# Splitting a norm's output into high and low parts: scale taken into the first product, the low part made on VectorE in one step

## The chip, the cores and the metric

The kernel runs on one core of a Trainium2 chip. The metric is the device time of one execution in microseconds (us). The core's engines run side by side and wait for one another by semaphores: TensorE (PE in the profile; PEld is its weight load), VectorE (DVE), ScalarE (ACT), GpSimd (POOL), and SyncE (SP), whose queue issues most DMAs.

## The reference, cut to what matters

The program is two transformer-like blocks over 512 tokens of width 1024 (256 of context, 256 of the sequence); the second block works on 256 tokens. All arithmetic is float32. What the change touches are the norms:

```python
def _rms_norm(x, gain):
    y = x * lax.rsqrt(jnp.mean(x * x, axis=-1, keepdims=True) + EPS)
    return y * gain

def _modulated_norm(h, gain, shift, scale):      # first block, 6 times
    return _rms_norm(h, gain) * (1.0 + scale) + shift

# second block, 3 times: rms_norm(h, norm_mix), rms_norm(h, norm_xattn), rms_norm(h, norm_mlp)
```

Each norm's output is multiplied by a large weight matrix (or several).

## The kernel before, in words

A float32 product is made of three TensorE products of rounded parts. Every operand `x` is kept as a high part `hi` (x rounded to the fp32r type) and a low part `lo = x - hi`; `three()` adds weights_lo·x_hi, weights_hi·x_lo and weights_hi·x_hi in PSUM (lines 231 to 233 of the profile). Weights come from memory in units of 512 KB (8 tiles of 128x128), issued by SyncE into 3 landing buffers; ScalarE makes their high part (`feed_act`, L214) and GpSimd their low part (`feed_pool`, L224), up to 4 units ahead of TensorE.

Data are held feature-major: 8 slices `d` of 128 features each, with 512 (or 256) tokens along the free axis. `linear()` starts a product with the first 1, 2 or 4 output tiles (`first`) slice by slice: for each `d` TensorE waits until slice `d` of the norm's low part is ready, and does 3 x `first` matmuls on it. The other output tiles follow without waiting for the norm. So the norm and the start of the next product overlap, at the pace of the slower.

A norm of 512 tokens goes like this. ScalarE squares, VectorE adds the squares, TensorE sums over features, ScalarE takes the root, VectorE the reciprocal (L492), and TensorE spreads the inverse root over all partitions into a PSUM bank (`spread_pe`, L469); it then does a few matmuls of no use (`busy_pe`, L420) that keep it occupied. From there, per slice `d`:

- VectorE `norm_x_dve` (L498): work = x * inverse root, 512 wide, one operand in PSUM
- ScalarE `norm_act` (L485): hi = work * scale + shift, in two halves (context tokens and sequence tokens have their own scale and shift)
- VectorE `norm_z_dve` (L504): work = work * scale + shift, in two halves, in SBUF
- GpSimd `norm_pool` (L520): lo = work - hi, 512 wide; TensorE waits for this

VectorE runs them in the order x0 x1 x2 z0 x3 z1 ... x7 z5 z6 z7 (`norm_dve`). The six norms of the first block (`norm00`, `norm01`, `norm02`, `norm10`, `norm11` on 512 tokens, `norm12` on 256) have a scale and a shift. The three of the second block (`norm mix`, `norm xattn`, `norm mlp`, 256 tokens) have a gain and no shift, so their pieces are one 256-wide piece. `norm00` is written out by hand in `start_dve`: its x products are made while the scale and shift themselves are still being computed from streamed weights (`ada_dve`); z follows when they are there. `norm_pool` sits in GpSimd's program between two stretches of `feed_pool`.

## Time and profile before

| | |
|---|---|
| time, median of 3 runs | 2959.94 us (2954.56 to 2963.52) |
| the profiled execution | 2956.96 us, span 2955.0 us |
| TensorE busy | 2811.4 us (95%) |
| VectorE busy | 1540.9 us (52%) |
| ScalarE busy | 1186.2 us (40%) |
| GpSimd busy | 1543.2 us (52%) |
| DMA | 381 MB, mean 129 GB/s |

"Busy" counts the time in which an engine executes instructions. The chain that ended last goes back from the last instruction, at each step to what released it; it lies on TensorE for 82% of the span. Matmuls are pipelined, so a row's duration (0.39 us for a 128x512 matmul) is longer than the distance from its start to that of the next. The chain is read together with the waits, which say for what an engine stood idle.

### The profile page before, as it was taken

To read this page: it belongs to the slowest core of one execution; us is meant where nothing else is said; L and a number is where in the kernel's file an instruction comes from. 1 tells how busy PE (TensorE), PEld (TensorE's weight loads), DVE (VectorE), ACT (ScalarE), POOL (GpSimd) and SP (SyncE) were. 2 spreads that over 40 slices of the span, in tenths; PEclk is the share of its full clock that TensorE was granted. 3 is DMA by queue.
4 is the path that set the end of the run, shared out by engine and by line. 5 is a ranking of instruction groups with operands and counts; after the bars stand their busy time and mean duration, and the time that the engine had idled before them with its cause. 6 is when DMAs were issued, how large, how long until landed. Compare 5 with 4: busy or idle time off the path is not lost.

```text
span 2955.0 us, 52281 instructions
## 1 busy us (share of the span) xinstructions
PE 2811.4 (95%) x21638; PEld 2427.7 (82%) x21638; DVE 1540.9 (52%) x2922; ACT 1186.2 (40%) x2076; POOL 1543.2 (52%) x861
## 2 busy tenths in 40 slices
PE   7999999988889999999999998999998998998999
PEld 5888878877777788887888885799997898997999
DVE  4777235535554667316665136554284865723570
ACT  4222234324453322223222244544445465544553
POOL 4444453343324544444444452388884565696697
PEclk9999999999999999999999998999998999999999
DMA  6555322210001555324554225155553343354365
GB/s 256 203 198 200 99 76 82 89 58 3 4 3 51 174 176 178 128 93 144 178 182 156 93 89 100 57 195 190 173 186 101 109 142 108 108 164 136 116 199 164
DMA packets 106123, 381.05 MB, mean 129 GB/s; under 512 B 11392, under 2 KB 16800, under 8 KB 104608
## 3 DMA queue, kind: packets, MB, share of 16 engines
q1 hardware_dynamic: 87456, 310.60, 32.2%
q10 hardware_dynamic: 18432, 67.12, 6.5%
q8 instruction: 172, 2.82, 0.4%
q14 instruction: 63, 0.52, 0.1%
HBM read 373.47 MB, written 4.19 MB: 128 GB/s over the span
## 4 chain that ended last, share of the span: by engine, by line
PE 82%; DVE 8%; POOL 3%; ACT 3%; issue 2%; DMA 1%; SPq 0%; ACTq 0%; DVEq 0%
PE bank L231 23%; PE bank L232 22%; PE bank L233 22%; POOL weights_lo L224 2%; PE bank L822 2%; DVE norm_work L504 1%; PE upper_banks L1555 1%; DVE norm_work L498 1%; PE upper_banks L231 1%; PE upper_banks L232 1%; PE upper_banks L233 1%; DMA ada_first<-w_ada 1%; DVE square_sums L451 1%; PE bank L919 1%; PE upper_banks L838 1%
## 5 line engine op out<-in xcount | busy, mean ns | idle before, releaser
L224 POOL TENSOR_TENSOR weights_lo<-weights_landing,weights_hi 128x1024 fp32r<-128x1024 f32 x554 | 1338.5, 2423 | 1101.0 <-ACT weights_hi L214 1100.4
L214 ACT ACTIVATE weights_hi<-weights_landing 128x1024 fp32r<-128x1024 f32 x554 | 586.5, 1061 | 1235.2 <-PE bank L233 1112.7
L231 PE MATMUL bank<-normed_hi,weights_lo 128*128 128x512 f32 (+1 forms) x2664 | 912.2, 342 | 17.6 <-POOL normed_lo L520 11.9
L232 PE MATMUL bank<-normed_lo,weights_hi 128*128 128x512 f32 (+1 forms) x2664 | 900.9, 338 | 0.0
L233 PE MATMUL bank<-normed_hi,weights_hi 128*128 128x512 f32 (+1 forms) x2664 | 900.0, 338 | 0.0
L231 PEld LDWEIGHTS bank<-normed_hi,weights_lo 128*128 128x128 f32 x2664 | 502.3, 189 | 95.2 <-POOL normed_lo L520 27.6
L233 PEld LDWEIGHTS bank<-normed_hi,weights_hi 128*128 128x128 f32 x2664 | 502.1, 188 | 61.6
L232 PEld LDWEIGHTS bank<-normed_lo,weights_hi 128*128 128x128 f32 x2664 | 502.6, 189 | 58.4
L231 PE MATMUL bank<-hidden_hi,weights_lo 128*128 128x512 f32 (+1 forms) x960 | 329.1, 343 | 0.0
L232 PE MATMUL bank<-hidden_lo,weights_hi 128*128 128x512 f32 (+1 forms) x960 | 329.1, 343 | 0.0
L233 PE MATMUL bank<-hidden_hi,weights_hi 128*128 128x512 f32 (+1 forms) x960 | 329.1, 343 | 0.0
L572 DVE TENSOR_TENSOR hidden_lo<-silus,hidden_hi 128x512 fp32r<-128x512 f32 (+1 forms) x88 | 210.9, 2397 | 87.3 <-ACT hidden_hi L559 87.3
L625 DVE SCALAR_TENSOR_TENSOR residual<-bank,gate,residual 128x256 f32<-128x256 f32 x80 | 35.5, 479 | 358.3 <-PE bank L233 358.3
L231 PEld LDWEIGHTS bank<-hidden_hi,weights_lo 128*128 128x128 f32 x960 | 180.1, 188 | 24.3
L232 PEld LDWEIGHTS bank<-hidden_lo,weights_hi 128*128 128x128 f32 x960 | 180.1, 188 | 24.2
L233 PEld LDWEIGHTS bank<-hidden_hi,weights_hi 128*128 128x128 f32 x960 | 180.1, 188 | 24.2
L390 DVE CUSTOM_DVE_ANT_0 ada_products<-ada_rows,upper_banks,k_cond_pack 128x1024 f32<-128x1024 f32 x128 | 163.3, 1276 | 22.9 <-DMA ada_rows<-w_ada_rows 14.0
L390 DVE CUSTOM_DVE_ANT_0 ada_rows<-ada_rows,upper_banks,k_cond_pack 128x1024 f32<-128x1024 f32 x128 | 163.1, 1274 | 0.0
L570 DVE TENSOR_TENSOR silus<-silus,bank 128x512 f32<-128x512 f32 (+1 forms) x88 | 54.7, 621 | 183.7 <-PE bank L233 158.7
L520 POOL TENSOR_TENSOR normed_lo<-norm_work,normed_hi 128x512 fp32r<-128x512 f32 (+1 forms) x72 | 76.6, 1068 | 75.1 <-DVE norm_work L504 75.1
L1689 DVE SCALAR_TENSOR_TENSOR upper_banks<-gl,k_pack,upper_banks 128x255 f32<-128x255 f32 (+14 forms) x210 | 99.3, 473 | 7.4
L451 DVE TENSOR_TENSOR square_sums<-square_sums,squares 128x512 f32<-128x512 f32 (+1 forms) x48 | 67.3, 1402 | 35.9 <-ACT squares L443 35.9
(447 smaller groups left out, 3912.1 us busy)
## 6 DMA issues: line engine op xcount, KB each, us to landing
weights_landing<-w_up SPq DMA_DIRECT2D x176, 512.0 KB, 3.5
ada_rows<-w_ada_rows ACTq DMA_DIRECT2D x128, 512.0 KB, 4.3
weights_landing<-w_down SPq DMA_DIRECT2D x88, 512.0 KB, 3.4
weights_landing<-w_dn SPq DMA_DIRECT2D x33, 512.0 KB, 3.4
weights_landing<-w_mlp_up SPq DMA_DIRECT2D x32, 512.0 KB, 3.4
weights_landing<-w_mlp_down SPq DMA_DIRECT2D x32, 512.0 KB, 3.5
weights_landing<-w_gate SPq DMA_DIRECT2D x24, 512.0 KB, 3.4
weights_landing<-w_xbc SPq DMA_DIRECT2D x24, 512.0 KB, 3.5
```

Source lines behind the costliest of these rows:

```text
L214: k.nc.scalar.activation(k.WH[:, u % SLOTS, :], k.W[:, u % LANDS, :], ACT.Copy).then_inc(*k.AC.mark(("unit hi", u)))
L224: k.nc.gpsimd.tensor_tensor(k.WL[:, u % SLOTS, :], k.W[:, u % LANDS, :], k.WH[:, u % SLOTS, :].bitcast(F32), ALU.subtract).then_inc(*k.PO. ...
L231: nc.tensor.matmul(out, ll, rh, start=start, stop=False, skip_group_check=True)
L232: nc.tensor.matmul(out, lh, rl, start=False, stop=False, skip_group_check=True)
L233: return nc.tensor.matmul(out, lh, rh, start=False, stop=stop, skip_group_check=True)
L390: nc.vector.tensor_tensor_reduce(k.row[r % ROW_LANDS][:] if c else k.row_out[:], k.row[r % ROW_LANDS][:], k.upper[:, c * D:(c + 1) * D], 1 ...
L451: k.nc.vector.tensor_tensor(s, s, k.sq[:, d % 2, 0:tokens], ALU.add).then_inc(*k.DV.mark((st, "sum", d)))
L520: k.nc.gpsimd.tensor_tensor(lo(d), work(d), hi(d).bitcast(F32), ALU.subtract).then_inc(*k.PO.mark((st, "lo", d)))
L570: nc.vector.tensor_tensor(s, s, k.B[(2 * p + 1) % 4][:, 0:tokens], ALU.mult).then_inc(*k.DV.mark((st, "raw", p)))
L572: nc.vector.tensor_tensor(lo(p), s, hi(p).bitcast(F32), ALU.subtract).then_inc(*k.DV.mark((st, "lo", p)))
L822: mm = k.nc.tensor.matmul(bank[block(to), at + c * BLK:at + (c + 1) * BLK], lhs(rows, to, c), rhs(rows, to, c), start=True, stop=True)
L1689: nc.vector.scalar_tensor_tensor(y[:, a:LAT], x[:, 0:LAT - a], w[:, at, j:j + 1], y[:, a:LAT], ALU.mult, ALU.add).then_inc(*k.DV.mark(("co ...
```

## The change

For norms with scale and shift: VectorE's first step becomes work = (x * scale) * inverse root, in two halves, as one instruction each with the scale as a per-partition operand. ScalarE's high part is work + shift, and is marked and waited for by half. VectorE then makes the low part itself, (work + shift) - hi, as one instruction for each half; z is gone. GpSimd's program waits in that place until the last low part is made, and does nothing for the norm. VectorE's order is s0 s1 low0 s2 low1 ... s7 low6 low7. TensorE waits for VectorE's mark instead of GpSimd's (`norm_ready`).

For the three norms without shift: VectorE's first step takes the gain in, ScalarE rounds work, z is gone, and GpSimd makes lo = work - hi as soon as hi is there.

For `norm00` the products are no longer made ahead of the scale; all of it starts when the first scale is ready.

```diff
-def norm_act(k, act, st, work, hi, parts, when=None):
+def norm_act(k, act, st, work, hi, parts):
     for d in range(KT):
-        act.wait_ge(*k.DV.after(st, "x", d))
         for n, (a, b, scale, shift) in enumerate(parts):
-            k.nc.scalar.activation(hi(d)[:, a:b], work(d)[:, a:b], ACT.Identity, scale=scale(d),
-                                   bias=shift(d) if shift else 0.0).then_inc(...)
+            act.wait_ge(*k.DV.after(st, "scaled", d, n))
+            k.nc.scalar.activation(hi(d)[:, a:b], work(d)[:, a:b], ACT.Identity,
+                                   bias=shift(d) if shift else 0.0).then_inc(*k.AC.mark((st, "hi", d, n)))

-def norm_x_dve(k, dve, st, d, src, work, tokens, bank=5):
+def norm_scaled_dve(k, dve, st, d, src, work, parts, bank=5):
     if d == 0:
         dve.wait_ge(*k.PE.after(st, "spread"))
-    k.nc.vector.tensor_tensor(work(d), src(d), k.B[bank][:, 0:tokens], ALU.mult).then_inc(*k.DV.mark((st, "x", d)))
-
-def norm_z_dve(k, dve, st, d, work, parts):
-    dve.wait_ge(*k.AC.after(st, "hi", d))
     for n, (a, b, scale, shift) in enumerate(parts):
-        k.nc.vector.tensor_scalar(work(d)[:, a:b], work(d)[:, a:b], scale(d), shift(d) if shift else None, ALU.mult,
-                                  *((ALU.add,) if shift else ())).then_inc(...)
+        k.nc.vector.scalar_tensor_tensor(work(d)[:, a:b], src(d)[:, a:b], scale(d), k.B[bank][:, a:b], ALU.mult,
+                                         ALU.mult).then_inc(*k.DV.mark((st, "scaled", d, n)))
+
+def norm_low_dve(k, dve, st, d, work, hi, lo, parts):
+    for n, (a, b, scale, shift) in enumerate(parts):
+        dve.wait_ge(*k.AC.after(st, "hi", d, n))
+        k.nc.vector.scalar_tensor_tensor(lo(d)[:, a:b], work(d)[:, a:b], shift(d), hi(d)[:, a:b].bitcast(F32), ALU.add,
+                                         ALU.subtract).then_inc(...)

-def norm_dve(k, dve, st, src, work, tokens, parts, bank=5):
+def norm_dve(k, dve, st, src, work, hi, lo, tokens, parts):
     norm_r_dve(k, dve, st, tokens)
-    for d in range(KT + 2):
+    for d in range(KT + 1):
         if d < KT:
-            norm_x_dve(k, dve, st, d, src, work, tokens, bank)
-        if d >= 2:
-            norm_z_dve(k, dve, st, d - 2, work, parts)
+            norm_scaled_dve(k, dve, st, d, src, work, parts)
+        if d and st in MODULATED:
+            norm_low_dve(k, dve, st, d - 1, work, hi, lo, parts)
+
+MODULATED = ("norm00", "norm01", "norm02", "norm10", "norm11", "norm12")

 def norm_pool(k, pool, st, work, hi, lo):
+    if st in MODULATED:
+        pool.wait_ge(*k.DV.after(st, "lo", KT - 1))
+        return
     for d in range(KT):
-        pool.wait_ge(*k.DV.after(st, "z", d))
+        pool.wait_ge(*k.AC.after(st, "hi", d, 0))
         k.nc.gpsimd.tensor_tensor(lo(d), work(d), hi(d).bitcast(F32), ALU.subtract).then_inc(*k.PO.mark((st, "lo", d)))
...
     ada_dve(k, dve, 1)
-    for d in range(KT):
-        norm_x_dve(k, dve, "norm00", d, src, work, TOK)
     for u in range(2, ADA_FIRST):
         ada_dve(k, dve, u)
+    dve.wait_ge(*k.DV.after("ada scale", 0, 0))
     for d in range(KT):
-        norm_z_dve(k, dve, "norm00", d, work, modulated(k, 0, 0))
+        norm_scaled_dve(k, dve, "norm00", d, src, work, modulated(k, 0, 0))
+        if d:
+            norm_low_dve(k, dve, "norm00", d - 1, work, hi, lo, modulated(k, 0, 0))
+    norm_low_dve(k, dve, "norm00", KT - 1, work, hi, lo, modulated(k, 0, 0))
```

## Rows read from the trace of the kernel before

**Rows 1.** The page, part 1: busy time (share of the span) and instructions of each engine.

```profile
PE 2811.4 (95%) x21638; PEld 2427.7 (82%) x21638; DVE 1540.9 (52%) x2922; ACT 1186.2 (40%) x2076; POOL 1543.2 (52%) x861
```

**Rows 2.** Waits of PE: line waited for: us in total, times, longest.

```profile
PE bank L231 <- POOL normed_lo L520: 11.9, 26, 3.7
```

**Rows 3.** Stretches: length, busy time (instructions) per engine, PEclk the granted clock.

```profile
37.00:55.00 18.00, 14.86 (x65) 11.65 (x66) 12.04 (x16) 11.38 (x20) 14.23 (x10) 0.83 0.00 1
55.00:413.00 358.00, 358.00 (x1537) 287.60 (x1536) 197.81 (x260) 94.58 (x115) 155.23 (x65) 1.00 0.49 169
```

**Rows 4.** Timeline of DVE in norm01: start, length, engine, line, form, [idle before <-releaser].

```profile
417.64 1.88 DVE L498 TENSOR_TENSOR norm_work<-residual,upper_banks 128x512 f32<-128x512 f32 x3 [0.74 <-PE upper_banks L469]
419.50 0.73 DVE L504 TENSOR_SCALAR norm_work<-norm_work,scale,mod 128x256 f32<-128x256 f32 x2
420.75 1.30 DVE L504 TENSOR_SCALAR norm_work<-norm_work,scale,mod 128x256 f32<-128x256 f32 x2
```

**Rows 5.** Timeline of ACT and of POOL in norm01.

```profile
418.37 4.05 ACT L485 ACTIVATE normed_hi<-norm_work,mod,scale 128x256 fp32r<-128x256 f32 x8 [1.68 <-DVE norm_work L498]
...
420.31 1.27 POOL L520 TENSOR_TENSOR normed_lo<-norm_work,normed_hi 128x512 fp32r<-128x512 f32 x1 [8.73 <-DVE norm_work L504]
...
432.74 1.28 POOL L520 TENSOR_TENSOR normed_lo<-norm_work,normed_hi 128x512 fp32r<-128x512 f32 x1 [0.23 <-DVE norm_work L504]
```

**Rows 6.** Timeline of PE in norm01: occupying matmuls, slice 1, slice 7.

```profile
417.44 3.19 PE L420 MATMUL upper_banks<-k_cond_pack 128*128 128x256 f32 x14
...
423.47 0.50 PE L231 MATMUL bank<-normed_hi,weights_lo 128*128 128x512 f32 x1 [0.16 <-POOL normed_lo L520]
423.81 0.39 PE L232 MATMUL bank<-normed_lo,weights_hi 128*128 128x512 f32 x1
424.04 0.40 PE L233 MATMUL bank<-normed_hi,weights_hi 128*128 128x512 f32 x1
...
434.07 0.50 PE L231 MATMUL bank<-normed_hi,weights_lo 128*128 128x512 f32 x1
```

**Rows 7.** Timeline of DVE elsewhere: 256-wide three-operand instructions, PSUM source, then SBUF only.

```profile
2577.46 3.21 DVE L2219 SCALAR_TENSOR_TENSOR mem<-mem,k_pack,upper_banks 128x256 f32<-128x256 f32 x8
...
2265.83 1.52 DVE L1689 SCALAR_TENSOR_TENSOR cv<-gl,k_pack,cv 128x255 f32<-128x255 f32 x3
```

**Rows 8.** Timelines of DVE and PE in norm00.

```profile
36.67 0.18 DVE L345 SCALAR_TENSOR_TENSOR scale<-mod,k_cond_pack 128x16 f32<-128x16 f32 x1
...
40.15 0.79 PE L231 MATMUL bank<-normed_hi,weights_lo 128*128 128x512 f32 x1 [3.72 <-POOL normed_lo L520]
...
51.72 0.50 PE L231 MATMUL bank<-normed_hi,weights_lo 128*128 128x512 f32 x1
```

**Rows 9.** Timelines of DVE and PE in norm12 (256 tokens).

```profile
1907.14 1.08 DVE L498 TENSOR_TENSOR norm_work<-residual,upper_banks 128x256 f32<-128x256 f32 x3 [0.80 <-PE upper_banks L469]
...
1916.00 0.28 PE L231 MATMUL bank<-normed_hi,weights_lo 128*128 128x256 f32 x1
```

**Rows 10.** Timelines of DVE and POOL in norm mix (no shift).

```profile
2099.33 1.08 DVE L498 TENSOR_TENSOR norm_work<-residual,upper_banks 128x256 f32<-128x256 f32 x3 [0.52 <-PE upper_banks L469]
...
2100.76 0.72 POOL L520 TENSOR_TENSOR normed_lo<-norm_work,normed_hi 128x256 fp32r<-128x256 f32 x1 [3.88 <-DVE norm_work L504]
...
2105.59 2.22 POOL L520 TENSOR_TENSOR normed_lo<-norm_work,normed_hi 128x256 fp32r<-128x256 f32 x3 [0.23 <-DVE norm_work L504]
```

**Rows 11.** Timelines of POOL and PE in norm xattn (no shift).

```profile
2663.18 9.48 POOL L224 TENSOR_TENSOR weights_lo<-weights_landing,weights_hi 128x1024 fp32r<-128x1024 f32 x4 [2.09 <-ACT weights_hi L214]
...
2679.91 11.81 POOL L224 TENSOR_TENSOR weights_lo<-weights_landing,weights_hi 128x1024 fp32r<-128x1024 f32 x5
...
2682.33 0.50 PE L231 MATMUL bank<-weights_hi,mem_lo 128*128 128x512 f32 x1 [2.39 <-POOL weights_lo L224]
```

**Rows 12.** Timeline of PE around and after norm mlp (no shift).

```profile
2770.63 1.03 PE L420 MATMUL upper_banks<-k_cond_pack 128*128 128x256 f32 x4
...
2795.18 0.36 PE L231 MATMUL bank<-normed_hi,weights_lo 128*128 128x256 f32 x1 [0.68 <-POOL weights_lo L224]
```

**Rows 13.** Groups by form: a low part made on DVE inside the MLPs, count | busy, mean ns | idle.

```profile
L572 DVE TENSOR_TENSOR hidden_lo<-silus,hidden_hi 128x512 fp32r<-128x512 f32 x66 | 158.1, 2395 | 62.9 <-ACT hidden_hi L559 62.9
```

More of the change, by code:

```diff
@@ L517, in norm_pool, with norm_ready @@
+def norm_ready(k, st):
+    return lambda d: (k.DV if st in MODULATED else k.PO).after(st, "lo", d)
 def norm_pool(k, pool, st, work, hi, lo):
+    if st in MODULATED:
+        pool.wait_ge(*k.DV.after(st, "lo", KT - 1))
+        return
     for d in range(KT):
[L519 removed]
+        pool.wait_ge(*k.AC.after(st, "hi", d, 0))
         k.nc.gpsimd.tensor_tensor(lo(d), work(d), hi(d).bitcast(F32), ALU.subtract).then_inc(*k.PO.mark((st, "lo", d)))
@@ L691, in delta_pe @@
     linear(k, pe, st, "w_dn", DN_TILES, KT, lambda d: (k.n_hi[:, d, :], k.n_lo[:, d, :]), TOK, freed,
-           lambda d: k.PO.after("norm01", "lo", d), first=2, beside=beside)
+           norm_ready(k, "norm01"), first=2, beside=beside)
 def delta_act(k, act):
@@ L1706, in glu_pe @@
     freed = lambda n: None if n < 8 else k.AC.after("glu", "sig", (n - 8) // 2) if n % 2 else k.DV.after("glu", "ev", (n - 8) // 2)
-    linear(k, pe, "glu", "w_glu", 2 * KT, KT, both2(k), LAT, freed, lambda d: k.PO.after("norm mix", "lo", d), first=4, banks=8)
+    linear(k, pe, "glu", "w_glu", 2 * KT, KT, both2(k), LAT, freed, norm_ready(k, "norm mix"), first=4, banks=8)
 def glu_act(k, act):
@@ L2277, in cross_vq_pe @@
     linear(k, pe, "cross q", "w_xq", KT, KT, both2(k), LAT,
-           lambda n: k.AC.after("cross q", "ev", n - 4) if n >= 4 else k.AC.after("cross v", n // 2, n % 2), lambda d: k.PO.after("norm xattn", "lo", d),
+           lambda n: k.AC.after("cross q", "ev", n - 4) if n >= 4 else k.AC.after("cross v", n // 2, n % 2), norm_ready(k, "norm xattn"),
            first=1, beside=lambda n: cross_beside_pe(k, pe, n))
@@ L2469, in mlp2_pe @@
     freed = lambda n: k.DV.after("up2", "square", n - 8) if n >= 8 else None
-    linear(k, pe, "up2", "w_mlp_up", 4 * KT, KT, both2(k), LAT, freed, lambda d: k.PO.after("norm mlp", "lo", d), first=4, banks=8)
+    linear(k, pe, "up2", "w_mlp_up", 4 * KT, KT, both2(k), LAT, freed, norm_ready(k, "norm mlp"), first=4, banks=8)
     out_pe(k, pe, "down2", "w_mlp_down", 4 * KT, lambda d: (k.mh_hi[:, d, :], k.mh_lo[:, d, :]), LAT,
@@ L2540, in mlp_pe @@
     hi, lo = hidden(k, tokens)
-    up_pe(k, pe, st, "w_" + up, lambda d: (k.n_hi[:, d, a:TOK], k.n_lo[:, d, a:TOK]), tokens, lambda d: k.PO.after(norm, "lo", d))
+    up_pe(k, pe, st, "w_" + up, lambda d: (k.n_hi[:, d, a:TOK], k.n_lo[:, d, a:TOK]), tokens, norm_ready(k, norm))
     out_pe(k, pe, st + " down", "w_" + down, FT, lambda d: (hi(d), lo(d)), tokens, down_freed(k, st, st + " down"), down_ready(k, st), stat=after)
@@ L2625, in pe_program @@
     spread_pe(k, pe, "norm11", TOK)
-    window_project_pe(k, pe, swa, lambda d: k.PO.after("norm11", "lo", d), lambda n: None)
+    window_project_pe(k, pe, swa, norm_ready(k, "norm11"), lambda n: None)
     window_heads_pe(k, pe, swa)
@@ L2651, in pe_program, with norm_of_act @@
     mlp2_pe(k, pe)
-def norm_of_act(k, act, st, tokens, where, parts, when=None):
+def norm_of_act(k, act, st, tokens, where, parts):
     src, work, hi, lo = where
     rms_act(k, act, st, tokens)
-    norm_act(k, act, st, work, hi, parts, when)
+    norm_act(k, act, st, work, hi, parts)
 def act_program(k, act):
@@ L2662, in act_program @@
     start_act(k, act)
-    norm_act(k, act, "norm00", *first_norm(k, TOK)[1:3], modulated(k, 0, 0), k.DV.after("ada scale", 0, 0))
+    norm_act(k, act, "norm00", *first_norm(k, TOK)[1:3], modulated(k, 0, 0))
     mlp_act(k, act, "mlp00")
@@ L2700, in norm_of_dve @@
     src, work, hi, lo = where
-    norm_dve(k, dve, st, src, work, tokens, parts)
+    norm_dve(k, dve, st, src, work, hi, lo, tokens, parts)
 def dve_program(k, dve):
```

5 lines of the change are left out of this document (1 added, 4 removed).

## The prediction

> **What bounds the kernel now.** I read the page first: TensorE is busy for 95% of the span [rows 1]. Then the stretches: from one norm to the next it has no gap at all, 358.00 us busy of 358.00 [rows 3], so a norm that ends earlier moves everything behind it forward. Nothing there runs on a clock of its own: weights, their high and low parts and their DMAs are all released by work that moves too. Then the waits: TensorE waits for GpSimd's low part of a norm 26 times, 11.9 us in all [rows 2]. That understates what a norm costs, since a matmul behind a wait also starts its successor late: 0.34 us later (423.47 to 423.81) where the next pair is 0.23 apart [rows 6]. So I went to the timelines of the norms, where the end of the last slice decides, not the sum of waits.
>
> In norm01 VectorE's first x starts at 417.64 [rows 4], GpSimd's last low part ends at 432.74 + 1.28 = 434.02 [rows 5], and TensorE begins slice 7 at 434.07 [rows 6]. Eight slices took 16.4 us. The two z of a slice last 0.73 us when GpSimd is idle and 1.30 when it works [rows 4]: VectorE and GpSimd take turns, so x (0.60), the z pair and GpSimd's 1.27 to 1.28 don't overlap freely and a slice costs about 1.84 us. TensorE needs only 6 x 0.233 = 1.40 us for a slice, 1.51 if it had to wait for it. This pattern stands four times in the trace, at norm01, norm02, norm10 and norm11; the other norms are shorter.
>
> **Norms of 512 tokens with shift (four).** Removed: 8 x, 16 z on VectorE, 8 low parts on GpSimd. Added: 32 VectorE instructions of three operands, 256 wide. Their price: eight of this kind with a PSUM source took 3.21 us [rows 7]; with about 0.47 us for one alone this is (3.21 − 0.47)/7 = 0.391 us from start to start. With both tensors in SBUF three took 1.52 us [rows 7], (1.52 − 0.48)/2 = 0.52 apart, but each of those needs the result of the one before. In the new order no instruction needs its predecessor, so I take 0.391 for both kinds, and keep 0.52 as the upper end. For the lower end I have no row below 0.391 for this form.
>
> The last low part then ends at 31 x 0.391 + 0.47 = 12.6 us after the start, at 430.2 instead of 434.0. ScalarE doesn't hold it up: its halves come every 0.505 us (8 in 4.05, rows 5), 1.01 per slice against 1.56 from VectorE, and the first high half is there at 417.64 + 0.47 + 0.04 + 0.59 = 418.7, before the first low part wants it at 417.64 + 4 x 0.391 = 419.2. What is late next is TensorE itself. The first slice's low part is there at 417.64 + 5 x 0.391 + 0.47 = 420.1, but the occupying matmuls run to about 420.45 [rows 6]. From there blocks cost 1.40 where the wait is already met and 1.51 where not; VectorE delivers every 1.56. Followed slice by slice, slice 7 begins at 431.0 and ends at 432.4; before it ended at 434.07 + 0.11 + 1.40 = 435.6. Gain 3.1 us each, 12.4 us for four. Bounds: if waits cost TensorE nothing, 3.6 each; with 0.52 per instruction the last low part comes at 417.64 + 16.6 = 434.2, gain −0.2 each. GpSimd's new wait holds only its weight units, and it ends when the last low part ends, earlier than its own last low part did; ScalarE's weight units come behind its high parts, as before.
>
> The Trainium skill's page "VectorE: DVE Perf Modes", sections "The perf-mode tier table" and "Rules for kernel authors", speaks against the edit: a one-source float32 tensor_scalar runs two elements per cycle in SBUF, two-source ones one, and one should minimise the number of instructions. Its measured formula (N+151)/0.96 would make each new instruction 424 ns and the last low part end at 13.6 us, not 12.6; the gain of a norm would be about 2.8 us instead of 3.1.
>
> **norm00.** Here the 8 x were already hidden, and the products now come behind the scale, which is ready at 36.67 + 0.18 = 36.85 [rows 8]. That costs nothing only because the order is short: the first slice's low part ends at 36.9 + 2.4 = 39.3, TensorE started at 40.15 [rows 8]. VectorE ends at 36.9 + 12.6 = 49.5; TensorE began slice 7 at 51.72. TensorE's granted clock is 0.83 over this stretch [rows 3]: it has been idle before, and its first matmul takes 0.79 us [rows 8]. I let that slow start move along with it. Then TensorE gains the 0.75 us of the start and about 0.35 of waits later: 1.1 us. Bounds 0.3 to 1.9; at 0.52 per instruction it would lose 36.9 + 16.6 − 51.7 = 1.8.
>
> **norm12** (256 tokens, two VectorE instructions per slice). s0 at 1907.14 [rows 9], high part until 1908.24, low0 until 1908.75, then 0.78 per slice; the last low part waits for its high part and ends at about 1914.2. TensorE's own blocks with a wait are 0.81, so slice 7 begins at 1914.5 instead of 1916.00 [rows 9]. Gain 1.5 us (1.0 to 1.7).
>
> **The three norms without shift.** z goes, GpSimd starts behind the high part. norm mix: first low part at 2099.33 + 0.47 + 0.04 + 0.51 + 0.08 = 2100.43 instead of 2100.76 [rows 10]; TensorE needs 12 matmuls a slice and is then the slower one, gain 0.3. GpSimd's steps are 0.74 apart where VectorE leaves it alone (three in 2.22, rows 10) and were 0.97 with z between. norm xattn: GpSimd's weight units end at 2672.66, its eight low parts then take 5.9 us, to 2678.6 instead of 2679.91; TensorE stands idle 2.39 us for exactly the weight unit that follows [rows 11]. Gain 1.3, up to 2.4 if the next waits shrink too. norm mlp: TensorE's occupying matmuls run to about the time at which it starts the product, nothing there; its wait of 0.68 us at 2795.18 [rows 12] hangs on GpSimd's weight units, which come 1.5 us earlier. I take 0.3 (0 to 0.7).
>
> **Sum.** 12.4 + 1.1 + 1.5 + 0.3 + 1.3 + 0.3 = 16.9 us. The profiled execution took 2956.96 (span 2955.0 and 1.96 around it), so 2940.1. The median of the runs is 3.0 us higher, which gives 2943.0. I forecast 2941.
>
> **The rivals.**
> 1. *The new instructions don't overlap* (0.48 apart or more, as in the dependent rows). At 0.48 the last low part ends 15.4 us after the start: 1.0 us gained in each of four norms, 0.6 lost in norm00, 0.6 gained in norm12, 1.9 in the others, 6 in all: 2952. For it: the 0.52 of the SBUF form [rows 7], and the waits in front of every low part. Against: the waits are met long before.
> 2. *VectorE is held off by GpSimd* (slower). A low part on VectorE reads two SBUF tensors; the same subtraction in the MLPs lasts 2395 ns on average, while GpSimd makes weight parts [rows 13]. If GpSimd had weight work during a norm, a slice would cost 4 x 1.4 = 5.6 us (two low parts at 2.4, two products at 0.4) and a norm 8 x 3.8 = 30 us more: with five such norms about 3100. It decides from the first weight unit that GpSimd makes inside a norm. Against: GpSimd has been idle 8.73 us when the norm needs it [rows 5], and the new wait keeps it idle until the last low part.
> The Trainium skill's page "SBUF — State Buffer", section "Who interferes with whom", has the rule: a VectorE instruction with two SBUF inputs and a GpSimd one that reads SBUF exclude each other for a whole instruction. By that rule the trace agrees with the 2395 ns of rows 13, and the change is safe only through GpSimd's wait.
> 3. *TensorE pays nothing for its waits, and the weight supply behind the norms profits more*: 4 x 3.6 + 1.5 + 1.7 + 0.5 + 2.4 + 0.7 = 21, giving 2937.
> 4. *The gain is given back* in the stages that wait for GpSimd, ScalarE or DMA: a third of it lost, 2947 to 2952.
>
> **How the numbers follow.** Forecast 0.68; rival 1 0.12; rival 2 0.04; rival 3 0.08; rival 4 0.05; something slower that I don't see 0.03. Runs of one kernel spread by about 4.5 us around the median. The range 2933 to 2953 takes in the forecast with this spread, rival 3, and most of rivals 1 and 4. A measurement can tell 0.3%, 8.9 us, from no change; the line for faster is 2951. Faster: forecast, rival 3, half of rival 4 and a little of rival 1, 0.80. Same: 0.14. Slower: 0.06.
>
> **What would show it.** Right: in norm01 32 three-operand instructions about 0.39 apart, the last ending 12.6 us after the first; TensorE's slice 7 about 13.4 us after VectorE's start instead of 16.4; no GpSimd instruction inside a norm with shift; TensorE's wait before the weight unit of norm xattn down from 2.39 to about 1.1. Wrong: starts 0.48 or more apart; any low part near 2.4 us; or the norms shorter as forecast and the span not.

## The result

The kernel after takes 2942.10 us, median of 4 runs (2938.66 to 2946.09), the kernel before 2959.51 (2954.56 to 2963.52). The ratio is 0.9942, with a 95% interval of 0.9922 to 0.9963. The profiled execution took 2943.61 us, its span is 2941.5, 13.5 us less than before. The interval ends below 1: the kernel after is faster, by 0.4 to 0.8%.

The page of after, part 1, beside [rows 1]: VectorE has 34 us less to do and GpSimd 60; TensorE has the same matmuls and stands idle less.

```profile
PE 2813.5 (96%) x21638; PEld 2435.2 (83%) x21638; DVE 1506.7 (51%) x2938; ACT 1177.8 (40%) x2076; POOL 1483.2 (50%) x813
```

The groups of after by form (line, engine, form, count | busy, mean ns | idle before) show what a norm is now made of. ScalarE makes the high parts; on VectorE one kind of instruction is left, twice.

```profile
L483 ACT ACTIVATE normed_hi<-norm_work,mod 128x256 fp32r<-128x256 f32 x88 | 39.9, 503 | 30.9 <-DVE norm_work L497 30.9
L504 DVE SCALAR_TENSOR_TENSOR normed_lo<-norm_work,mod,normed_hi 128x256 fp32r<-128x256 f32 x88 | 38.4, 478 | 0.4 <-ACT normed_hi L483 0.4
L497 DVE SCALAR_TENSOR_TENSOR norm_work<-residual,scale,upper_banks 128x256 f32<-128x256 f32 x88 | 38.0, 474 | 3.5 <-PE upper_banks L469 3.5
```

The waits of TensorE in after, which answer to [rows 2] (11.9 us in 26 waits for the low part). Of the waits long enough for this list (over 0.15 us) one is left, and it is norm00's start.

```profile
PE bank L231 <- DVE normed_lo L504: 3.0, 1, 3.0
```

norm01 in the timelines of after (start, length, engine, line, form), VectorE first, which answers to [rows 4].

```profile
419.04 1.66 DVE L497 SCALAR_TENSOR_TENSOR norm_work<-residual,scale,upper_banks 128x256 f32<-128x256 f32 x4 [0.74 <-PE upper_banks L469]
420.62 0.88 DVE L504 SCALAR_TENSOR_TENSOR normed_lo<-norm_work,mod,normed_hi 128x256 fp32r<-128x256 f32 x2
421.41 0.87 DVE L497 SCALAR_TENSOR_TENSOR norm_work<-residual,scale,upper_banks 128x256 f32<-128x256 f32 x2
...
430.07 1.67 DVE L504 SCALAR_TENSOR_TENSOR normed_lo<-norm_work,mod,normed_hi 128x256 fp32r<-128x256 f32 x4
```

ScalarE and GpSimd in the same norm [rows 5]. GpSimd makes nothing here: it stood for 18.85 us, and its weight units go on when the last low part is made.

```profile
419.56 1.71 ACT L483 ACTIVATE normed_hi<-norm_work,mod 128x256 fp32r<-128x256 f32 x4 [1.47 <-DVE norm_work L497]
...
431.82 7.15 POOL L224 TENSOR_TENSOR weights_lo<-weights_landing,weights_hi 128x1024 fp32r<-128x1024 f32 x3 [18.85 <-DVE normed_lo L504]
```

TensorE [rows 6]: the occupying matmuls, the first matmul of the product, the starts of slices 6 and 7, and the first matmul behind slice 7.

```profile
418.84 3.19 PE L420 MATMUL upper_banks<-k_cond_pack 128*128 128x256 f32 x14
421.68 0.58 PE L231 MATMUL bank<-normed_hi,weights_lo 128*128 128x512 f32 x1
...
431.00 0.50 PE L231 MATMUL bank<-normed_hi,weights_lo 128*128 128x512 f32 x1
...
432.50 0.39 PE L231 MATMUL bank<-normed_hi,weights_lo 128*128 128x512 f32 x1
...
433.91 0.39 PE L231 MATMUL bank<-normed_hi,weights_lo 128*128 128x512 f32 x1
```

The reading is simple. VectorE's instructions start 0.394 us apart (four from 419.04 to 420.62), and the last low part ends at 430.07 + 1.67 = 431.74, 12.70 us after the first start; before it was 16.4. Slice 7 starts 13.46 us after VectorE's start and is done at 14.87 us, against 17.9 before (slice 7 began at 434.07, and with 0.11 + 1.40 us for a block that had to wait, the prediction's price, it was done at 435.6). A first matmul of 0.50 us marks a block that had to wait a little; slice 7 begins with one of 0.39, so its data were there.

**Where the 17 us went.** The kernel's stages can be measured from one norm's spread (L469) to the next. Two such stages in the timeline of TensorE, before:

```profile
952.09 0.65 PE L469 MATMUL upper_banks<-k_cond_pack,rr 128*128 128x128 f32 x4
...
1334.45 0.65 PE L469 MATMUL upper_banks<-k_cond_pack,rr 128*128 128x128 f32 x4 [0.20 <-DVE rr L492]
```

and after:

```profile
948.75 0.65 PE L469 MATMUL upper_banks<-k_cond_pack,rr 128*128 128x128 f32 x4
...
1328.01 0.65 PE L469 MATMUL upper_banks<-k_cond_pack,rr 128*128 128x128 f32 x4 [0.20 <-DVE rr L490]
```

382.36 us became 379.26. The table has these stages for all kernels profiled ("before 2" is the kernel before and "again" the kernel after, once more each; the other names are the experiments below). A stage is named by the norm with which it starts, since its gain falls in it.

| kernel | 00 | 01 | 02 | 10 | 11 | 12 | mix | xattn | mlp | span |
|---|---|---|---|---|---|---|---|---|---|---|
| before | 391.37 | 535.14 | 382.36 | 382.37 | 189.67 | 192.37 | 569.49 | 100.18 | 186.47 | 2955.0 |
| before 2 | 392.49 | 535.73 | 382.39 | 382.37 | 189.00 | 192.43 | 573.69 | 98.82 | 186.26 | 2958.0 |
| after | 392.59 | 530.40 | 379.26 | 379.26 | 186.85 | 192.19 | 568.91 | 101.49 | 184.79 | 2941.5 |
| again | 392.16 | 532.51 | 379.29 | 379.26 | 186.66 | 192.38 | 566.85 | 98.29 | 184.85 | 2937.2 |
| four | 390.87 | 534.37 | 379.28 | 379.30 | 186.10 | 192.50 | 571.55 | 101.91 | 186.54 | 2948.5 |
| noshift | 391.20 | 534.83 | 382.46 | 382.41 | 190.05 | 192.45 | 567.15 | 100.98 | 185.23 | 2952.6 |
| halfway | 392.78 | 537.44 | 381.79 | 381.80 | 189.01 | 194.30 | 569.36 | 101.88 | 185.04 | 2958.7 |
| poolwork | 392.99 | 533.31 | 381.01 | 380.99 | 187.61 | 192.20 | 570.82 | 101.08 | 186.34 | 2951.4 |
| n00old | 391.25 | 533.52 | 379.26 | 379.26 | 186.38 | 190.73 | 568.70 | 100.80 | 185.04 | 2940.5 |
| warm | 389.70 | 535.43 | 379.27 | 379.25 | 186.75 | 192.38 | 567.41 | 100.98 | 184.66 | 2941.5 |
| first3 | 390.56 | 538.01 | 378.41 | 378.41 | 185.56 | 194.98 | 566.68 | 101.29 | 184.69 | 2943.7 |
| alldve | 390.67 | 531.81 | 379.26 | 379.26 | 186.71 | 190.61 | 566.82 | 99.87 | 185.57 | 2936.1 |
| best | 388.41 | 529.23 | 378.43 | 378.44 | 186.05 | 192.38 | 569.80 | 99.48 | 184.42 | 2932.6 |

The stages 02 and 10, in which TensorE has no gap behind the norm, repeat to 0.1 us, and it is there that a claim about a norm of 512 can be held to a tenth. Stages 01, mix and xattn, with their many small steps, differ by 0.6 to 4.2 us between two executions of one program (xattn 98.29 and 101.49 for the kernel after, mix 569.49 and 573.69 for the kernel before). A difference of that size in one of those stages alone says nothing.

norm01 and norm11 can be held to a tenth too, up to the next place where TensorE spreads inverse roots. For norm01 that is L688 in before (L699 in after), before and then after:

```profile
587.13 1.09 PE L688 MATMUL upper_banks<-k_cond_pack,rr 128*128 128x128 f32 x8 [1.26 <-DVE rr L786]
```

```profile
585.47 1.09 PE L699 MATMUL upper_banks<-k_cond_pack,rr 128*128 128x128 f32 x8 [1.26 <-DVE rr L797]
```

With norm01's own spread at 416.95 and 418.35 these are 170.18 and 167.12 us. In all profiles the old norm01 takes 170.2 to 170.3 and the new one 167.1, and norm11, measured in the same way, 34.7 to 34.8 and 31.6 (halfway and poolwork, whose norms are neither, lie between). So each of the four norms gained 3.1 us, and what stages 01 and 11 show beside that comes from behind their norm.

### The profile page after: what moved, and what is told of

The parts are those of the page before. It is cut to its first block, busy times and chain, and to the rows that moved or that the text cites. A ratio compares the mean times of both kernels' runs of the same rounds, so it can differ in the third digit from the quotient of the medians.

```text
span 2941.5 us, 52255 instructions
## 1 busy us (share of the span) xinstructions
PE 2813.5 (96%) x21638; PEld 2435.2 (83%) x21638; DVE 1506.7 (51%) x2938; ACT 1177.8 (40%) x2076; POOL 1483.2 (50%) x813
## 4 chain that ended last, share of the span: by engine, by line
PE 85%; DVE 6%; POOL 3%; ACT 3%; issue 2%; DMA 1%; SPq 0%; ACTq 0%; DVEq 0%
PE bank L231 23%; PE bank L233 23%; PE bank L232 23%; POOL weights_lo L224 2%; PE bank L833 2%; PE upper_banks L1566 1%; PE upper_banks L232 1%; PE upper_banks L231 1%; PE upper_banks L233 1%; DMA ada_first<-w_ada 1%; DVE square_sums L451 1%; PE bank L930 1%; PE upper_banks L849 1%; PE upper_banks L810 1%; PE upper_banks L420 1%
## 5 line engine op out<-in xcount | busy, mean ns | idle before, releaser
L231 PEld LDWEIGHTS bank<-normed_hi,weights_lo 128*128 128x128 f32 x2664 | 503.9, 189 | 77.4 <-DVE normed_lo L504 10.2
L631 DVE TENSOR_TENSOR residual<-residual,bank 128x256 f32<-128x256 f32 x24 | 9.8, 415 | 130.3 <-PE bank L233 130.3
```

The lines of the kernel that those rows point to most:

```text
L231: nc.tensor.matmul(out, ll, rh, start=start, stop=False, skip_group_check=True)
```

## The experiments

**The change again, timed more often.** No edit (again), beside one more profiled execution of the kernel before (base2, "before 2" in the table).

> The changed kernel once more, without any edit. Theory: the gain is 17 us (ratio about 0.994), and the stage lengths from norm01 on repeat to about 0.2 us. What is open is the slow stretch of TensorE's clock at the first slices of norm00 (until 46.9 us in the changed kernel, until about 43.1 before) and the one after norm xattn (2679 to 2685). If they are chance, another profile shows other lengths, up to 3 us off; if they belong to the change, they repeat.

> The kernel before once more, without any edit, for a second profile. It shows which stage lengths repeat: from norm02 to norm10 and from norm10 to norm11 382.4 within 0.1; the stage with the delta heads (norm01 to norm02) within some 3 us, the ones behind norm mix and norm xattn within 2.

2939.25 us (2933.51 to 2944.89), ratio 0.9935 (0.992 to 0.995) against 2959.69 for the kernel before; its one profiled execution gave 2959.89. The gain is 17 to 20 us. The stages repeat less well than expected. Between after and again 02, 10, 11, 12 and mlp agree to 0.2 us, but 01 and mix differ by 2.1 and xattn by 3.2; between the two of before mix differs by 4.2, where 2 was expected. The slow start of norm00 came back (14 slow matmuls after 13), but it is long in one of the two executions of before as well (see *warm*).

**Only part of the norms.** The old helpers are put back beside the new ones, and a tuple says which norms use them; norm00's own program goes with it.

```diff
+OLD = ("norm00", "norm12", "norm mix", "norm xattn", "norm mlp")                      # four
+OLD = ("norm00", "norm01", "norm02", "norm10", "norm11", "norm12")                    # noshift
+OLD = ("norm00",)                                                                     # n00old
 def norm_dve(...):
+    if st in OLD:
+        for d in range(KT + 2):
+            if d < KT:
+                norm_x_dve(k, dve, st, d, src, work, tokens)
+            if d >= 2:
+                norm_z_dve(k, dve, st, d - 2, work, parts)
+        return
```

*four* changes only the four norms of 512 tokens behind norm00.

> Only norm01, norm02, norm10 and norm11 as in the change, the other five as before. Theory (the sum of the prediction): 4 x 3.1 = 12.4 us less than before, and each of these four shows VectorE starts 0.39 apart. Rival, the gain sits mainly in the other norms or in the weight supply behind them: 8 us or less.

2948.47 us, ratio 0.9966 (0.9953 to 0.9978), 10.1 us less (6.5 to 13.9). The stages 02 and 10 are 3.1 us shorter, norm01 and norm11 by the shorter measure 3.1 each (167.10 and 31.59), and stages 00, 12 and mlp keep their old length. The term of 12.4 us stands.

*noshift* changes only norm mix, xattn and mlp.

> Only the three norms without shift as in the change, the six with shift as before. Theory: 0.3 + 1.3 + 0.3 = 1.9 us less than before; TensorE's wait in norm xattn of 2.39 us falls to 0.7, as in the changed kernel, and its wait of 0.68 after norm mlp goes. Rival, what is won in norm xattn is lost again in the next wait, for cross_squares, which stands on a DMA and is followed by a slow clock: 0 us.

2955.19 us, ratio 0.9982 (0.997 to 0.9994), 5.3 us less (1.8 to 8.9). That is more than the 1.9 us of the prediction, but its interval reaches down to it. Stage 02 stays at 382.46. TensorE's first wait in norm xattn fell to 0.72 us, as expected, but stage xattn (100.98) is no shorter than before's 98.82 and 100.18. Stage mlp loses 1.1 us: with the old norm mlp it takes 186.26 to 186.54 (before, before 2, four), with the new one 184.42 to 185.23 in eight profiles; poolwork, with the same norm mlp and 186.34, is an exception that I can't explain, and alldve (185.57) has another norm mlp.

*n00old* is the change, with norm00 as before.

> The changed kernel with norm00 as before (x made ahead, z, low part on GpSimd). Theory of the prediction: 1.1 us more than the changed kernel. Rival, as the changed kernel's one trace reads: no difference, since the slow clock of the first slices takes back what VectorE gives.

2942.37 us, ratio 0.994 (0.9924 to 0.9955): as the whole change, where 1.1 us more was expected, which is less than medians can tell. From the end of the scale to the next product (L364) it takes 53.09 − 36.71 = 16.38 us, before 53.23 − 36.85 = 16.38, and the change 16.56 (after) and 16.64 (again). So against these two, norm00 brought nothing. The other execution of before took longer, 16.99 (below), and beside that one norm00 did gain 0.4.

**Why norm00 brought so little (warm).** VectorE and TensorE in after (beside [rows 8]): the scale, TensorE's first matmul, the last slow one and the next, and the end of the group.

```profile
37.89 0.17 DVE L345 SCALAR_TENSOR_TENSOR scale<-mod,k_cond_pack 128x16 f32<-128x16 f32 x1
...
40.60 0.79 PE L231 MATMUL bank<-normed_hi,weights_lo 128*128 128x512 f32 x1 [2.96 <-DVE normed_lo L504]
...
45.89 0.63 PE L231 MATMUL bank<-normed_hi,weights_lo 128*128 128x512 f32 x1
46.32 0.53 PE L232 MATMUL bank<-normed_lo,weights_hi 128*128 128x512 f32 x1
...
54.62 1.58 PE L364 MATMUL upper_banks<-k_cond_pack,cond 128*128 128x128 f32 x13
```

The same in before: the slow matmuls end at 42.87, and at 50.20 TensorE waits for a slice again.

```profile
42.87 0.58 PE L231 MATMUL bank<-normed_hi,weights_lo 128*128 128x512 f32 x1
...
50.20 0.50 PE L231 MATMUL bank<-normed_hi,weights_lo 128*128 128x512 f32 x1
...
53.23 1.03 PE L364 MATMUL upper_banks<-k_cond_pack,cond 128*128 128x128 f32 x8
```

In both, TensorE comes out of a wait of 3 to 4 us at 1.2 GHz, the lower of its two clock levels (its matmuls start 0.43 us apart; later, at 2.4 GHz, 0.23). A matmul of 0.55 us or longer is called slow here. In before the data came at 1.84 us a slice, and TensorE caught up with them, so the slow ones were partly hidden. In after TensorE is the slower one, no block behind 46.32 begins with a wait, and each further slow matmul moves the end by about 0.2 us. *warm* keeps TensorE busy over the wait.

```diff
     ada_turn_pe(k, pe, ADA_FIRST - 1)
+    busy_pe(k, 6)
```

> The changed kernel, with six 128x256 matmuls of no use between TensorE's last work on the scale and its first slice of norm00 (about 2.6 us at the low clock; they end before the first low part is there). Theory, norm00 gained nothing because TensorE ran its first 13 to 14 matmuls at the low clock while it, and no longer the low parts, set the pace: with the clock up some 2.5 us earlier the time from the scale to the rows of the first MLP falls from 16.6 to about 15.2 us. Rival, the clock rises at the same time whatever TensorE did before: still 16.6.

TensorE in warm: the busy matmuls, the first of the product, and the next product.

```profile
36.20 2.84 PE L420 MATMUL upper_banks<-k_cond_pack 128*128 128x256 f32 x12
39.30 0.50 PE L231 MATMUL bank<-normed_hi,weights_lo 128*128 128x512 f32 x1 [0.27 <-DVE normed_lo L504]
...
51.66 1.91 PE L364 MATMUL upper_banks<-k_cond_pack,cond 128*128 128x128 f32 x16
```

The group takes 51.66 − 36.77 = 14.89 us, and none of its matmuls is slow. `busy_pe(k, 6)` stands in the trace as 12 matmuls. They were expected to run at the lower level and to bring the clock up; in fact the granted clock from 36 to 46 us is 1.00, against 0.52 in after and 0.66 in before, so with them it never fell. The rival, that the clock rises at the same time whatever TensorE did before, is out. With the other kernels that have two first tiles here, the count of slow matmuls orders the lengths:

| norm00 | slow matmuls: from the scale to L364 |
|---|---|
| as before | 7: 16.38 (before), 8: 16.38 (n00old), 10: 16.62 (noshift), 11: 16.82 (four), 12: 16.99 (before 2) |
| changed | 0: 14.89 (warm), 10: 15.84 (alldve), 13: 16.56 (after), 14: 16.64 (again) |

At 10 slow matmuls the change is 0.8 us shorter, by one execution of each. The count differs between executions whatever the kernel: 7 and 12 in two of the kernel before, and with other forms of the product or the norm 8 (first3), 9 (poolwork) and 13 (halfway). after and again had many of them; whether that is chance or comes with the edit, these few executions don't decide. The whole kernel warm takes 2943.03 us, ratio 0.9944 (0.9932 to 0.9956): its 1.7 us drown in the scatter of stage 01 (535.43 here, 530.40 and 532.51 in after and again). Stage 00 is shorter, 389.70 against 392.59 and 392.16; the part of that beyond 1.7 lies ahead of the end of the scale.

**Which half of the edit does it (halfway).** The product with the scale stays; the low part is made the old way, with an addition on VectorE and the subtraction on GpSimd.

```diff
-        k.nc.vector.scalar_tensor_tensor(lo(d)[:, a:b], work(d)[:, a:b], shift(d), hi(d)[:, a:b].bitcast(F32), ALU.add, ALU.subtract)
+        k.nc.vector.tensor_scalar(work(d)[:, a:b], work(d)[:, a:b], shift(d), None, ALU.add)    # marks z
...
-        pool.wait_ge(*k.DV.after(st, "lo", KT - 1)); return
+        pool.wait_ge(*k.DV.after(st, "z", d))                                                    # then lo = work - hi
```

> The changed kernel, but in the six norms with shift VectorE only adds the shift to work (in SBUF, in place) and GpSimd subtracts, as before the change. So the scale is taken into the first product and nothing else of the norms with shift is changed; the three norms without shift are as in the change. Theory, the gain comes from taking GpSimd out of the slice: here a slice still costs 1.28 + 0.56 = 1.84 us, norm00 begins later and loses 1.7, the norms without shift keep their part: 2955 to 2959, some 15 more than the changed kernel. Rival, the gain comes from the new first product and from the shorter lead (two slices instead of three): near 2945.

2957.98 us, ratio 0.9989 (0.9978 to 0.9999), inside the 2955 to 2959 expected, and far from the rival's 2945. Stages 02 and 10 lose 0.57 us of 3.1. VectorE and GpSimd in its norm01:

```profile
420.34 0.61 DVE L504 TENSOR_SCALAR norm_work<-norm_work,mod 128x256 f32<-128x256 f32 x2
420.87 0.87 DVE L497 SCALAR_TENSOR_TENSOR norm_work<-residual,scale,upper_banks 128x256 f32<-128x256 f32 x2
421.65 1.06 DVE L504 TENSOR_SCALAR norm_work<-norm_work,mod 128x256 f32<-128x256 f32 x2
```

```profile
424.58 1.30 POOL L528 TENSOR_TENSOR normed_lo<-norm_work,normed_hi 128x512 fp32r<-128x512 f32 x1 [0.49 <-DVE norm_work L504]
426.37 1.30 POOL L528 TENSOR_TENSOR normed_lo<-norm_work,normed_hi 128x512 fp32r<-128x512 f32 x1 [0.49 <-DVE norm_work L504]
```

A slice costs 1.79 us, almost the old 1.84: GpSimd's 1.30 and the 0.49 in which it waits for VectorE, which in turn is held up beside it (the pair lasts 0.61 alone and 1.06 beside GpSimd). So 2.5 of the 3.1 us come from taking the low part away from GpSimd, and 0.6 from the scale in the product and the shorter order that goes with it. The number of VectorE instructions is not what decides: both kernels have four a slice.

**Is GpSimd's silence needed (poolwork).** The change, and for every slice GpSimd also subtracts the high part from itself into a buffer that nobody reads (lines below it move by one or more).

```diff
     if st in MODULATED:
+        for d in range(KT):
+            pool.wait_ge(*k.AC.after(st, "hi", d, ...))
...
+            k.nc.gpsimd.tensor_tensor(t, hi(d).bitcast(F32), hi(d).bitcast(F32), ALU.subtract).then_inc(...)
         pool.wait_ge(*k.DV.after(st, "lo", KT - 1))
```

> The changed kernel, and GpSimd makes one subtraction of two SBUF operands (512 or 256 wide, both the high part of the slice) into a scratch buffer that nobody reads, for every slice of the six norms with shift, as soon as the slice's high part is there. Nothing waits for it but GpSimd's own next step. Theory (VectorE's low part, with two SBUF tensors, and GpSimd's subtraction exclude each other): a slice of 512 tokens costs 1.28 (GpSimd) + 0.79 (two low parts) = about 2.07 us instead of 1.58, the stages from norm02 to norm10 and from norm10 to norm11 are some 3 to 4 us longer than 379.3, about as long as before the change or longer. Rival, they don't exclude each other for this form: 379.3, and the low parts stay at 478 ns.

2951.85 us, ratio 0.9978 (0.9966 to 0.9989): 6.3 us less than before, so about two thirds of the gain are gone. Stages 02 and 10 are 1.7 us longer than in after, where 3 to 4 were expected; norm12's gain is gone as well (its stage takes 192.20), and so is stage mlp's, which the edit doesn't touch. In norm10 VectorE (the first two pairs of low parts, and the last four) and GpSimd:

```profile
1334.62 2.43 DVE L505 SCALAR_TENSOR_TENSOR normed_lo<-norm_work,mod,normed_hi 128x256 fp32r<-128x256 f32 x2
1336.97 0.86 DVE L498 SCALAR_TENSOR_TENSOR norm_work<-residual,scale,upper_banks 128x256 f32<-128x256 f32 x2
1337.76 0.87 DVE L505 SCALAR_TENSOR_TENSOR normed_lo<-norm_work,mod,normed_hi 128x256 fp32r<-128x256 f32 x2
...
1345.64 2.45 DVE L505 SCALAR_TENSOR_TENSOR normed_lo<-norm_work,mod,normed_hi 128x256 fp32r<-128x256 f32 x4
```

```profile
1334.55 2.22 POOL L534 TENSOR_TENSOR scratch<-normed_hi 128x512 f32<-128x512 f32 x2 [7.57 <-ACT normed_hi L484]
1338.46 1.06 POOL L534 TENSOR_TENSOR scratch<-normed_hi 128x512 f32<-128x512 f32 x1 [1.69 <-ACT normed_hi L484]
```

The pair of low parts that meets two GpSimd instructions (2.22 us from 1334.55) lasts 2.43 us instead of 0.88. Then the two fall into step: each of the next GpSimd instructions (1.06 us, one every 1.58) begins as a pair of low parts ends (1338.46, the pair until 1337.76 + 0.87 = 1338.63) and runs beside the products, which read PSUM and stay at 0.86. One more collision comes at the end. The norm takes 15.0 us instead of 12.7. That VectorE and GpSimd exclude each other is shown. The expectation's 2.07 us for every slice is not: it took each slice for a collision, and what it costs depends on who meets whom.

The Trainium skill's page "SBUF — State Buffer", section "Who interferes with whom", says that a VectorE instruction with two SBUF inputs and a GpSimd one that reads SBUF contend, and that a VectorE instruction with at most one SBUF input, outside certain fast modes, doesn't. The run agrees, with 2.43 against 0.88 us for a pair of low parts and 0.86 for a pair of products, whose second input lies in PSUM.

**The same on VectorE without shift (alldve).** norm mix, xattn and mlp make their low part on VectorE too, with a tensor_tensor, and GpSimd does not stop for them.

```diff
+        if not shift:
+            k.nc.vector.tensor_tensor(lo(d)[:, a:b], work(d)[:, a:b], hi(d)[:, a:b].bitcast(F32), ALU.subtract)
...
+            if st[:5] != "norm ":
                 pool.wait_ge(*k.DV.after(st, "lo", KT - 1))
```

> The changed kernel, and the three norms without shift make their low part on VectorE too (work - hi, one instruction); GpSimd doesn't stop for them and goes on with weight units. Theory: in norm xattn GpSimd's five weight units come 5.6 us earlier, TensorE's wait of 0.73 us goes, but each low part can be held for a weight unit's 2.4 us; nobody needs them before 10 us later, so this costs nothing: up to 1 us less between norm mix and norm mlp. In norm mix and norm mlp TensorE is the slower one, and its first slice is there 0.25 us earlier. Together about 1 us less than the changed kernel, 2939 to 2942. Rival, GpSimd's weight units come into norm mix or norm mlp and hold VectorE's low parts: 2 to 5 us more.

2940.25 us (2933.07 to 2949.01), ratio 0.994 (0.9923 to 0.9958), the same as the change. In norm mix and norm mlp TensorE's first slice is there 0.35 us earlier (1.91 us after the spread instead of 2.26), but stage mlp is 0.7 us longer, with a new wait of 0.80 for a weight unit. In norm xattn TensorE's wait, expected to go, grew from 0.73 to 1.16 us: GpSimd's five units began at 2660.96 after 5.94 us of waiting for ScalarE's high parts, so GpSimd was free and had nothing to do. There a first low part on VectorE met a weight unit of GpSimd (three units from 2647.84 to 2655.01), a later one did not:

```profile
2652.88 2.42 DVE L505 TENSOR_TENSOR normed_lo<-norm_work,normed_hi 128x256 fp32r<-128x256 f32 x1 [0.93 <-ACT normed_hi L483]
...
2655.61 0.41 DVE L505 TENSOR_TENSOR normed_lo<-norm_work,normed_hi 128x256 fp32r<-128x256 f32 x1
```

2.42 us for an instruction of 0.41: this is the mechanism of rival 2 in one row, with the price that the prediction gave it.

**What is late next behind VectorE (first3).** In a norm of the change VectorE delivers a slice every 1.58 us and TensorE uses 1.40 on it. With three first tiles in the four up products (the first products of the MLPs, behind norm00, norm02, norm10 and norm12) it uses 9 x 0.233 = 2.1 and would never wait.

```diff
-    linear(k, pe, st, stream, 2 * FT, KT, x, tokens, up_freed(k, st), ready, first=2, beside=beside)
+    linear(k, pe, st, stream, 2 * FT, KT, x, tokens, up_freed(k, st), ready, first=3, beside=beside)
```

(The weight units held ahead for these products go from 2 to 3 tiles too.)

> The changed kernel, and the up products of the four MLPs start with three output tiles beside the norm instead of two (weights packed to match). Theory, after the change VectorE (1.575 us a slice) is still slower than TensorE (1.40): with three tiles TensorE needs 2.10 a slice and never waits; norm02 and norm10 gain 8 x 0.175 = up to 1.4 us each, less the deeper start, norm12 0.5, norm00 (bound by TensorE and its slow clock) 0: 2 to 3 us less than the changed kernel in the stages behind norm02, norm10 and norm12. Rival, the third bank taken makes the first tiles behind wait for ScalarE: the stages get longer.

2945.66 us, ratio 0.9954 (0.994 to 0.9968), not the 2 to 3 us less than the change that were expected. Stages 02 and 10 lose another 0.85 us, of up to 1.4. But stage 12 is 2.6 us longer, where TensorE, 256 wide, waits for ScalarE to read a bank, which was the rival:

```profile
1912.82 0.40 PE L231 MATMUL bank<-normed_hi,weights_lo 128*128 128x256 f32 x1 [3.26 <-ACT silus L567]
```

**Both together (best).** busy_pe as in warm, and three first tiles behind norm00, norm02 and norm10, two behind norm12.

> The changed kernel with the six warming matmuls ahead of norm00's product and three first tiles in the three MLPs of 512 tokens; the MLP behind norm12 keeps two, since with three TensorE stood 3.26 us for ScalarE's silu there. Theory: 1.7 us less up to norm01 from the clock, 0.9 less in the stage from norm02 to norm10 and the same from norm01's side of norm00, about 3 us less than the changed kernel: 2937 to 2940, and the time from the scale to the first MLP's rows near 15. Rival, they don't add up: TensorE is already the slower one in norm00, so only one of the two counts there: 2 us less.

2937.06 us (2934.61 to 2948.2), ratio 0.9935 (0.9917 to 0.9952), span 2932.6. Stage 00 is 388.41, 02 and 10 are 378.43 and 378.44. By the two stages that repeat it is 1.7 us faster than the change, and stage 00 is 4 us shorter. Since three tiles put more matmuls ahead of L364, norm00 is compared from the end of the scale to norm01's spread: 380.29 in after, 378.61 in warm, 377.55 in best, so there the two gains add up, 1.7 + 1.1, and the rival (only one of them counts) is out. The medians (2937.1 against 2939.3 and 2942.1) can't show such a difference, since their runs overlap. It is the fastest of these kernels by its stages; that it is by its time is not shown.

## Why the prediction was right

The forecast was 2941 us; the runs gave 2942.10 and 2939.25. The sum itself led to 2940.1 from the profiled execution and to 2943.0 from the median; 2941 was picked between them without a reason given, and the result doesn't tell them apart. By the stages of two executions each (mean of after and again, less mean of before and before 2) the terms came out so:

| term | predicted | stage | at its own place |
|---|---|---|---|
| norm01, 02, 10, 11 | −12.4 | −4.0, −3.1, −3.1, −2.6 = −12.8 | −3.1 each |
| norm00 | −1.1 | +0.4 | −0.1 by the means, −0.8 at 10 slow matmuls |
| norm12 | −1.5 | −0.1 | −1.8 |
| norm mix | −0.3 | −3.7 (scatter of 4) | −0.7 |
| norm xattn | −1.3 | +0.4 (scatter of 3) | −1.7 |
| norm mlp | −0.3 | −1.5 | −1.0, and a later wait of 0.68 gone |

**The four norms** held in every step. The distance between instructions is 0.394 us (0.391 taken), with PSUM and with SBUF sources; the last low part ends after 12.70 (12.6), slice 7 starts after 13.46 (13.4), the gain is 3.1 (3.1). ScalarE didn't hold it up; its instruction even became shorter, 591 to 503 ns, with no scale operand, which I hadn't counted and which hid in idle time. The dependent SBUF rows of [rows 7] were rightly put aside: low parts with both tensors in SBUF, none of which needs the one before, start as close together as the products do. The Trainium skill's formula on the page "VectorE: DVE Perf Modes", which the page gives for a tensor_tensor and which the prediction used for the new form (424 ns each, a norm of 13.6 us), is met by neither number: an instruction lasts 474 to 478 ns by itself and begins 394 ns behind the last, and the norm took 12.70 us.

**norm00: the step that failed** is "I let that slow start move along with it". It took for granted that the slow start is the same in every execution, and that TensorE loses to it what it lost before. But the kernel before had 7 slow matmuls in one execution and 12 in the other (16.38 and 16.99 us from the scale to L364), and the kernel after 13 and 14 (16.56 and 16.64). TensorE, now the slower of the two, pays about 0.2 us for each beyond ten. The means differ by 0.1 us; what stage 00 shows beyond that, and the other way, lies ahead of the scale (from the spread to its end 11.3 and 11.8 us before, 12.3 and 11.8 after). With 7 of them the change would take between 15.84 − 3 x 0.2 = 15.2 us (the slope from 10 to 14 in the table above) and 14.89 + 7 x 0.095 = 15.6 (the slope from 0 to 10), 0.8 to 1.1 less than before's 16.38. So the 1.1 was about right for an equal start (0.8 at 10 slow matmuls), the start wasn't equal, and next to nothing of it was left.

**norm12** gained more at its place than forecast: its 48th matmul starts 8.2 to 8.5 us after the spread instead of 10.1 to 10.2. VectorE in after:

```profile
1894.59 0.87 DVE L497 SCALAR_TENSOR_TENSOR norm_work<-residual,scale,upper_banks 128x256 f32<-128x256 f32 x2 [0.53 <-PE upper_banks L469]
...
1901.04 0.48 DVE L504 SCALAR_TENSOR_TENSOR normed_lo<-norm_work,mod,normed_hi 128x256 fp32r<-128x256 f32 x1 [0.18 <-ACT normed_hi L483]
```

Yet the stage is as long as before. The stretches of TensorE inside it, before and then after (length, busy time and instructions of PE, PEld, DVE, ACT, POOL, granted clock, DMA share, GB/s):

```profile
1920.00:1970.00 50.00, 50.00 (x431) 50.00 (x430) 26.41 (x20) 24.66 (x37) 45.67 (x20) 1.00 0.61 202
```

```profile
1920.00:1970.00 50.00, 50.00 (x427) 50.00 (x426) 25.61 (x18) 24.29 (x36) 45.01 (x20) 1.00 0.63 196
```

TensorE has no gap in either and the clock is 1.00 in both, but it does 427 matmuls instead of 431 (again has 426), 0.1171 us apart instead of 0.1160. Over a stage of 190 us that is 1.7 us, the whole gain. The pace goes over the whole stage and differs between executions, and with it the stages sort themselves: old norm12 at 431, 192.37 to 192.50 (before, before 2, four, noshift); changed at 431, 190.73 and 190.61 (n00old, alldve); changed at 427, 192.19 to 192.38 (after, again, warm, best). So norm12 is worth 1.75 us, and in both executions of the change the slow pace hid it. The other three fit: halfway (427, 194.30) and poolwork (431, 192.20) have their 48th matmul only after 10.3 and 9.9 us, and first3 (431, 194.98) has the wait of 3.26. The slow pace came in five of the nine profiles with an edited norm12 and in none of the four with the old one, which chance alone could do; whether the edit decides stays open, and I have no experiment on it.

**The norms without shift.** norm mix and mlp gained 0.7 and 1.0 us up to their 96th matmul (13.5 after the spread instead of 14.2 and 14.5) where I had taken 0.3: in after and again the first matmul comes 2.26 us after the spread instead of 2.68 and 2.74 to 2.94, and the waits behind it are gone too, which I had counted little or not at all. In mlp the wait of [rows 12] is gone as well, and the stage is 1.5 us shorter. norm xattn did what was said at its place. GpSimd's low parts and weight units in after, beside [rows 11], and TensorE's wait:

```profile
2659.49 5.63 POOL L531 TENSOR_TENSOR normed_lo<-norm_work,normed_hi 128x256 fp32r<-128x256 f32 x8
2665.07 11.81 POOL L224 TENSOR_TENSOR weights_lo<-weights_landing,weights_hi 128x1024 fp32r<-128x1024 f32 x5
```

```profile
2667.52 0.50 PE L231 MATMUL bank<-weights_hi,mem_lo 128*128 128x512 f32 x1 [0.73 <-POOL weights_lo L224]
```

That wait went from 2.39 to 0.73 us, and it repeats: 2.38 to 2.39 in the three profiles with the old norm, 0.70 to 0.77 in the nine that have the new one as in the change. The next wait, for cross_squares, grew from 2.32 to 2.89 in this pair, but that is no reaction to the change: it is 2.32, 3.19 and none with the old norm and 1.94 to 3.26 with the new one. What reached the end can't be told: the stage scatters by 3 us.

**The sum** was right, 16.9 against 17.2 by the means of two spans each (2956.5 and 2939.35), and the rivals are settled so. Rival 1 (no overlap) is out, at 0.394 apart. Rival 2 is real in its mechanism (poolwork, alldve, the 2.42 us) and absent from the change, since GpSimd waits. Rival 3 is out in its mechanism: TensorE still pays 0.1 us for each block that waits, and the four norms gained 3.1 each and not 3.6; its total of 21 us lies inside the interval of again. Rival 4 is not seen: no wait that grew with the change is shown. But the sum owes something to luck: norm00 and norm12 showed 2.9 us less than forecast in their stages and xattn 1.7 less, and this was made up by norm mlp (1.2 more than forecast) and by stage mix (3.4 more, in a stage that scatters by 4).

## What to carry to other kernels

When VectorE and GpSimd make a value in turns, look first at whether they exclude each other. One engine that does it alone, with more and narrower instructions that don't depend on the one before, can be faster than both, as long as the other is kept out. Price an instruction by the distance between two starts, not by its length. And when a faster producer hands the pace to TensorE, every weakness of TensorE in that stretch, a slow clock above all, is paid from then on.

## What the hardware showed that I had not expected

- TensorE at a granted clock of 1.00, with no gap, did 256-wide matmuls 0.1160 us apart in some executions and 0.1171 in others, over a whole stage.
- A ScalarE instruction of 256 columns lasts 503 ns without a scale read from SBUF, and 591 with it.
- VectorE and GpSimd excluded one another only when they met: with GpSimd's instruction at 1.06 us and a period of 1.58 they fell into step after the first collision (2.43 us), and the pairs between were as fast as alone (0.87).
- After a wait of 3 to 4 us TensorE did its first 7 to 14 matmuls 0.43 us apart, the count different from one execution to the next, of one kernel too (7 and 12). With 12 matmuls of no use in the wait the granted clock stayed at 1.00 and there were none.
